# Two reorderings in the second block: low parts of two weight chunks around the query norms, and the router's first products ahead of the experts

## What is computed

```
hc, hx = context and latent tokens, scaled and shifted       # 256 + 256 tokens
proj   = h @ w_in            # parts: q, k|v, xbc (1536 columns), dt, z
q      = rope(rms_norm(q))   # 16 heads
xs|B|C = silu(conv5(xbc));  dt = softplus(dt_raw + dt_bias)
y      = state space scan of (xs, B, C, dt), both directions
o      = attention(q, k, v);  x = layer_norm(alpha*x + g_a * [y, o] @ w_out)
h      = x * (1 + sc_f) + sh_f
g      = h @ w_rg + b_rg;  e = h @ w_re + b_re           # router: 4 + 16 columns
weights of the 16 experts = top group, then top 2 of its 4 experts
out    = layer_norm(alpha*x + g_f * sum_e (silu(h@gate_e) * (h@up_e) * weight_e) @ down_e)
```

## Time and profile before

| what | us |
|---|---|
| median of 3 runs | 1785.45 (1785.32 to 1785.61) |
| the profiled execution, its own time | 1781.5 |
| its span, first to last instruction | 1779.5 |
| PE busy | 1640.4 (92%) |
| DVE busy | 1142.4 (64%) |
| ACT busy | 798.8 (45%) |
| POOL busy | 251.5 (14%) |
| mean granted TensorE clock | 0.954 |

### The profile page before, as it was taken

The page is one execution under the profiler, slowest core; times in us unless marked ns, Lnnn a source line. Parts: engine busy times, 40 slices in busy tenths (PEclk is TensorE's granted clock), DMA queues, the critical chain, the costliest instruction groups (busy, mean ns, idle before and its releaser), DMA issues. The chain is left out here.

```text
span 1779.5 us, 27095 instructions
## 1 busy us (share of the span) xinstructions
PE 1640.4 (92%) x10920; PEld 1412.4 (79%) x10920; DVE 1142.4 (64%) x1530; ACT 798.8 (45%) x1099; POOL 251.5 (14%) x287
## 2 busy tenths in 40 slices
PE   7999999899998999999899989898998868999996
PEld 5887898799976888889799976684565657899995
DVE  4669997566645669997566634767448564455555
ACT  4355554455533465554555424333227433343331
POOL 0200004144301200004254200103220000000000
PEclk9999999999999999999999999899869978999998
DMA  6554454465553545445465554221100222454541
GB/s 259 184 196 170 185 190 178 173 241 215 188 206 141 199 170 200 166 167 189 178 237 213 190 189 175 71 95 71 48 1 1 92 98 95 166 187 172 186 187 71
DMA packets 40123, 282.09 MB, mean 159 GB/s; under 512 B 4816, under 2 KB 5072, under 8 KB 6864
## 3 DMA queue, kind: packets, MB, share of 16 engines
q1 hardware_dynamic: 38432, 273.15, 41.4%
q10 hardware_dynamic: 1584, 7.42, 1.2%
HBM read 279.50 MB, written 1.05 MB: 158 GB/s over the span
## 5 line engine op out<-in xcount | busy, mean ns | idle before, releaser
L429 DVE TENSOR_TENSOR ring_low<-ring,sb_hi 128x2048 fp32r<-128x2048 f32 x116 | 271.0, 2336 | 180.4 <-ACT sb_hi L424 180.2
L424 ACT ACTIVATE sb_hi<-ring 128x2048 fp32r<-128x2048 f32 x116 | 222.5, 1918 | 278.2 <-DMA ring<-weights 121.2
L578 PE MATMUL psum<-sb_hS,sb_hi 128*128 128x256 f32 x704 | 202.2, 287 | 9.7 <-DVE ring_low L429 9.5
L581 PE MATMUL psum<-sb_hS,sb_hi 128*128 128x256 f32 x704 | 198.8, 282 | 0.0
L582 PE MATMUL psum<-sb_hS,ring_low 128*128 128x256 f32 x704 | 198.1, 281 | 0.0
L840 PE MATMUL psum<-sb_hfT,ring_low 128*128 128x256 f32 x704 | 196.8, 280 | 0.0
L1848 DVE TENSOR_TENSOR sb_split<-ring,sb_split 128x2048 fp32r<-128x2048 f32 x48 | 109.9, 2292 | 104.3 <-ACT sb_split L1843 104.3
L2229 PE MATMUL psum<-sb_hfS,sb_split 128*128 128x256 f32 x512 | 146.1, 285 | 6.1 <-DVE sb_hfS L2834 3.9
L578 PEld LDWEIGHTS psum<-sb_hS,sb_hi 128*128 128x128 f32 x704 | 133.1, 189 | 20.1 <-DVE ring_low L429 13.0
L2232 PE MATMUL psum<-sb_hfS,sb_split 128*128 128x256 f32 x512 | 145.4, 284 | 0.0
L2233 PE MATMUL psum<-sb_hfS,sb_split 128*128 128x256 f32 x512 | 145.4, 284 | 0.0
(11 more groups left out here) (435 smaller groups left out, 4103.7 us busy)
## 6 DMA issues: line engine op xcount, KB each, us to landing
ring<-weights SPq DMA_DIRECT2D x256, 1024.0 KB, 4.8
sb_rows_ffn<-rows ACTq DMA_DIRECT2D x4, 512.0 KB, 4.3
sb_rows_mix<-rows ACTq DMA_DIRECT2D x2, 1024.0 KB, 7.5
sb_rows<-rows ACTq DMA_DIRECT2D x1, 2048.0 KB, 9.8
sb_x<-x_in SPq DMA_DIRECT2D x2, 512.0 KB, 5.8
sb_y<-ctx_in SPq DMA_DIRECT2D x1, 1024.0 KB, 5.6
out<-sb_x SPq DMA_DIRECT2D x2, 512.0 KB, 2.6
sb_const<-const SPq DMA_DIRECT2D x1, 711.0 KB, 13.3
```

The lines of the kernel that those rows point to most:

```text
L424: act.activation(hi_of(n), ring[:, c % SLOTS, :], ACT.Copy).then_inc(hi_ready, 1)
L429: eng.tensor_tensor(low_of(n), ring[:, SPLIT_CHUNKS[n] % SLOTS, :], hi_of(n).bitcast(F32), ALU.subtract).then_inc(lo_dve, 1)
L578: mm = pe.matmul(out, hi[:, k, bs], hS[:, 0, k, :], start=(k == 0), stop=False)
L581: pe.matmul(out, hi[:, k, bs], hS[:, 1, k, :], start=False, stop=False)
```

## The change

In the inner projection, the low part of chunk 6 moves on DVE from behind `q_norm(1)` to between the two query norms. The high and low parts of chunk 7 move ahead of the dt chain: on ACT behind the k and v copies, on DVE directly behind `q_norm(1)`. At the experts, `strips("routeS")` moves on PE from behind gate 0 to ahead of the wait for the last low part of `hf`, with waits for the four drains of `hf`; `strip_sums("route")` moves from n = 2 to n = 1; ACT copies `routeS` ahead of the high part of expert chunk 2; DVE makes the low part of expert chunk 3 behind the router's logits and not ahead of them. No instruction is added or removed apart from waits.

```
--- before.py
+++ after.py
@@ -2210,6 +2210,10 @@
                 pe.wait_ge(x_normed, t + 1)
                 for c in range(2):
                     transpose4(("hf", c, t), [x[:, t, (4 * c + i) * P:(4 * c + i + 1) * P] for i in range(4)])
+            for t in range(TT):
+                for c in range(2):
+                    jobs.wait_drained(pe, ("hf", c, t))
+            strips("routeS", "w_r", hf)
             pe.wait_ge(h_lo, 4)
             pe.sem_inc(hid_used, 2)
 
@@ -2257,8 +2261,6 @@
             def experts(step):
                 for n, (part, e) in enumerate(MOE_ORDER):
                     if isinstance(step, int) and n == 1:
-                        strips("routeS", "w_r", hf)
-                    if isinstance(step, int) and n == 2:
                         strip_sums("route", wx[:, 0, 0:T], "routeS", TT, 20)
                     if isinstance(step, int) and n == 4:
                         weights_of_tokens()
@@ -2343,13 +2345,14 @@
             act.activation(expA, R("alog"), ACT.Exp).then_inc(a_ready, 1)
             for i in range(SEQ_TILES):
                 copy_out(("kv", i), kv[:, i, :])
+            weight_hi(act, 7)
             act.wait_ge(dt_neg, 1)
             act.activation(tmp_b[:, :, :], tmp_b[:, :, :], ACT.Exp).then_inc(dt_exp, 1)
             act.wait_ge(dt_u, 1)
             act.activation(tmp_a[:, :, :], tmp_a[:, :, :], ACT.Ln).then_inc(dt_ln, 1)
             for b in range(DX + 1):
                 if b < DX:
-                    if b % 2 == 0 and b < DX - 2:
+                    if b % 2 == 0 and 2 <= b < DX - 2:
                         weight_hi(act, 7 + b // 2)
                     jobs.wait_filled(act, ("xbc", b))
                     dst = xbc_xs[:, b, :] if b < 8 else bcf[:, b - 8, :]
@@ -2450,8 +2453,8 @@
             for c in range(2):
                 jobs.wait_drained(act, ("hf", c, 1))
                 high_part(1, c)
+            copy_out("routeS", wx[:, 0, 0:T], jobs.out("routeS")[:, 0:T])
             split_hi(act, 0, 2)
-            copy_out("routeS", wx[:, 0, 0:T], jobs.out("routeS")[:, 0:T])
 
             def silu(step, e):
                 wait_expert(act, step, "G", e, "filled")
@@ -2594,8 +2597,9 @@
             weight_lo(dve, 5)
             dve.wait_ge(params, 32)
             q_norm(0)
+            weight_lo(dve, 6)
             q_norm(1)
-            weight_lo(dve, 6)
+            weight_lo(dve, 7)
             jobs.wait_filled(dve, "dt")
             jobs.drain(dve.tensor_tensor(dtr[:, :, :], jobs.out("dt")[:, 0:128].rearrange("p (i h) -> p i h", i=4),
                                          bc(R("dtb").unsqueeze(1), [P, 4, 32]), ALU.add), "dt")
@@ -2837,7 +2841,6 @@
             dve.sem_inc(hid_hi, 2)
             dve.sem_inc(hid_ready, 2)
             split_lo(dve, 0, 2)
-            split_lo(dve, 0, 3)
 
 
             jobs.wait_filled(dve, "route")
@@ -2863,6 +2866,7 @@
             chain(dve.tensor_reduce(es[:, :, :], r32[:, :, :, :].rearrange("p t g e -> p t e g"), AX_X, ALU.add))
             chain(dve.tensor_reduce(r2b, es[:, :, :], AX_X, ALU.max))
             dve.tensor_tensor(es[:, :, :], es[:, :, :], bc(r2b.unsqueeze(2), [P, 2, 4]), ALU.subtract).then_inc(r_logits, 1)
+            split_lo(dve, 0, 3)
             dve.wait_ge(r_exp, 2)
             chain(dve.tensor_reduce(gs, r8a[:, :, :], AX_X, ALU.add))
```

## The result

| | before | after |
|---|---|---|
| median, us | 1785.51 (1785.32 to 1785.61, 4 runs) | 1769.86 (1767.49 to 1770.73, 4 runs) |
| profiled execution, us | 1781.5 | 1770.73 |
| its span, us | 1779.5 | 1768.6 |
| mean granted clock | 0.954 | 0.955 |

The ratio is 0.9911, with a 95% interval of 0.9898 to 0.9923: the change saves 15.6 us where 9.6 were forecast. The time lies 0.6 us under the range.

What follows compares the result with a forecast made beforehand. PE bounds the kernel, so gains come where it stands still or runs at the low clock. The sum -8.3 - 1.3 = -9.6 us gives 1771.9 for the profiled execution, plus 3.95 carried over: 1775.9, range 1770.5 to 1781.5.

Steps and rivals of the forecast that it cites:

- The stop of 8.2 us: Ahead of xbc 0, PE waits for the low part of chunk 6, late only by DVE's order; removing it: -8.2 us.
- The new stop ahead of xbc 3: Inner projection: PE waits from 1143.9 to 1145.8 for taps 0 to drain a region, +1.9 us, with no fall in clock.
- the twelve blocks: Xbc in the inner projection ends 8.3 us earlier: 8.2 + 2.5 - 1.9 - 0.5, bounds -6.7 to -8.7.
- Part two: Router's strips moved at the start of the experts: worth -1.3 us, between -0.5 and -2.1.
- The moved copy and low parts at the experts: ACT's strips copy delays chunk 2, and chunk 3's low part moves behind the logits; both hidden, with no cost.
- the router's earlier result: Router's chain on DVE ends at about 1483, but PE asks for its result only at 1491.89: buys nothing.
- The stop of 0.5 us at xbc 4: Inner projection: PE waits for the low part of chunk 8, behind ACT's Silu table load and high part, +0.5 us.
- The strips: Ahead of gate 0 they fit PE's wait with nothing to spare: 0 to 0.5 us, taken as +0.2.
- the half microsecond: At gate 0 the full clock returns sooner, -0.5 us; lost if products of 32 columns fare like transposes.
- the clock in the scan comes out otherwise: Rival: scan's clock shifts with fine timing; gain to 1771.9 (chance 0.11), or loss to 1782 to 1784 (0.08 with small gain).
- the lucky case: In the scan, the clock comes out better by 3.95 us, giving 1771.9; chance 0.11.
- The carried 3.95 us: Median of the runs lies 3.95 us above the profiled execution; this was added to 1771.9, giving 1775.9.

Runs made afterwards that it cites:

- both pairs: First pair: the profiled executions of the kernel before and the changed kernel, 1781.5 and 1770.73 us; second pair: e0_before and e1_after, one after the other on one chip.
- e8_lo6: The kernel before with only the low part of chunk 6 moved between the query norms: 1781.83 us, ratio 0.9981.
- e0_before: The kernel before, unchanged, run and traced again: 1785.1 us, ratio 1.0.
- e1_after: The changed kernel, unchanged, run and traced again: 1769.4 us, ratio 0.9912 to the kernel before.
- e2_part1: The kernel before with only the part of the diff that concerns chunks 6 and 7: 1771.52 us, ratio 0.993.
- e3_part2: The kernel before with only the part of the diff that concerns the router: 1783.46 us, ratio 0.999.
- e4: The kernel before with one unused 1.25 us multiply on DVE ahead of the copy of the cumulative sums: 1786.13 us, ratio 1.0006.
- e7: The changed kernel with two unused multiplies, 2.5 us, on DVE ahead of the copy of the cumulative sums: 1776.37 us, ratio 0.995 to the kernel before.
- e10_router_early: The changed kernel with the router's two transposes one chunk earlier, ahead of up 1: 1774.23 us, ratio 0.9934 to the kernel before.
- e6: The changed kernel with one unused 1.25 us multiply on DVE ahead of the copy of the cumulative sums: 1776.56 us, ratio 0.9946 to the kernel before.
- e9: The changed kernel with the first taps of block 0 ahead of the dt chain, on ACT and DVE: 1770.18 us, ratio 0.9919 to the kernel before.
- e11: The changed kernel with the edits of both e9 and e10_router_early: 1767.72 us, ratio 0.9903 to the kernel before.
- e12: The changed kernel with the second half of the dense z products and the ACT copies of z one unit later: 1773.3 us, ratio 0.9928 to the kernel before.
- e13: The kernel of e11 with the second half of the dense z products and the ACT copies of z one unit later: 1770.4 us, ratio 0.9915.

## Why the prediction was wrong

**Right, and shown.** The stop of 8.2 us was the order on DVE and nothing else, and it went. The clock of 1.00 was kept through it. The new stop ahead of xbc 3 measured 1.65 us for 1.9 worked out, and did not cost the clock. From the first matmul of block 2 to the first of xbc it took 8.3 us less in both pairs, and all of xbc came out 8.0 to 9.0 us shorter for 8.3; the twelve blocks themselves took 69.5 us before in the first pair and 68.5 in the second, which makes the difference. That chunk 7 had to move is shown by e8_lo6. The moved copy and low parts at the experts were hidden, and the router's earlier result bought nothing. Part two alone measured 1.3 us (1784.73 to 1783.46) for 1.3, within an interval of 0.2 to 3.4, so that this match is partly luck.

**Small errors.** The stop of 0.5 us at xbc 4 was charged for a table load that ACT does while it waits. The strips were charged 0.2 us and cost none. The full clock came back at gate 0 1.2 us sooner in the first pair and 3.3 us sooner in the second, which is worth half of that, 0.6 to 1.7 us for the 0.5 in the sum. PE at the start of gate 0, at the low clock, in e0_before, e1_after, e2_part1 and e3_part2:

```profile
1467.30:1472.00 4.70, 4.70 (x22) 0.51 0.02 5
...
1453.30:1454.70 1.40, 1.36 (x6) 0.50 0.06 18
...
1454.10:1458.90 4.80, 4.80 (x22) 0.50 0.02 5
...
1468.20:1469.50 1.30, 1.25 (x6) 0.50 0.06 19
```

So the half microsecond that products of 32 columns might have failed to win was won. The strips bring this, and not the earlier start of the stage: e2_part1 has the stage 13.2 us sooner than e0_before and no strips ahead of it, and the low clock lasts as long; e3_part2 has the strips and a start within 0.9 us of that of e0_before, and it is short. In the traces part two gives 1.9 to 2.7 us. Together the touched stages give 10.6 to 10.9 us, a miss of 1.0 to 1.3 on 9.6.

**What failed** is the term that the sum put at nothing, the clock in the scan. The sum of 9.6 us has no share for it, and the step that was to cover it, the rival "the clock in the scan comes out otherwise", had its gain and its chance too small. Its mechanism is the one that the runs show. I priced the lucky case by the 3.95 us between the profiled execution and the median, which came from elsewhere. The runs show 5.8 us for the scan, from the cumulative sums to the scores (123.0 us in e0_before, 117.2 in e1_after), of which the units give 7.8 and the stage ahead of them takes back 2.0. With 5.8 in place of 3.95 the lucky case is 1785.45 - 9.6 - 5.8 = 1770.05, and the measured median is 1769.86. The rows at hand gave a bound for the price: 26 us at clock 0.50 with PE busy throughout is up to 13 us of loss. The range, with its end at 1770.5, was cut for a price of 4.

I also gave the lucky change a chance of only 0.11, as if the long stretch were a property of the kernel. The delays of e4 to e7 leave the work of the units as it is and change when the scan begins, and with two multiplies the stretch of the kernel before falls away. So the start of the scan takes part in deciding it, and a shift of 8 us made the old stretch a poor guide. It does not decide alone: e10_router_early, unchanged ahead of the experts, mostly has the long one. Of the eight traces here in which xbc is over about 8 us sooner and the z products are in their place, four have the long stretch (the first of the changed kernel, e6, e7, e10) and four have not (e1, e2, e9, e11), so an even chance would have been nearer.

One reading of the rows was wrong as well. The stretches of rows 10 do not hold the same kinds of small products. PE from 1264 to 1287 us in the kernel before:

```profile
L1987 PE MATMUL psum<-ring,sb_hT 128*128 128x512 f32 x28 | 13.0, 616 | 0.0
```

These 28 products of 512 columns fill 13.0 of the 23 us, and from 1288 to 1314 there are none of them. So the rows did not show that fine timing alone decides; e12 and e13, which move half of such products, do change where the clock is low.

**The carried 3.95 us** was no constant either. The profiled execution of before had a fast block 1: it was over at 1072.6 us, and in the fourteen later traces at 1077.9 to 1081.3, with the same work. PE was busy there for 1005.5 us at a mean clock of 0.98 (7304 matmuls), and in e0_before for 1012.0 at 0.97 (7305), while its idle time was 67.1 and 66.2 us: the difference is the clock.

## What to carry to other kernels

Follow a removed stall through all queues to the next wait; that gave each of the touched stages here to within 1.3 us. Then look for long stretches in which PE is busy and the granted clock is 0.50: each is worth up to half its length, and a shift of 1 to 3 us ahead of it can win or lose a part of that (5.8 us here), so it belongs in the range with its full price. Count with it what the stage ahead gives back. A kernel with such a stretch has to be judged by several executions and by its stages, since one edit's own worth (here 10.6 us) and its time (15.6) can differ by half.

## What I had not expected of the hardware

- Added work can make a kernel faster. 2.5 us more on the critical path gave 1781.74 against 1784.79 us, ratio 0.9982 [0.9972, 0.9991], by a low-clock stretch in the scan that fell away (units of 75.3 us in e0_before, 73.8 with half the added work, 69.0 here).
- PE can be busy for 28.4 of 28.5 us at a mean clock of 0.52 (e0_before, 1290 to 1318.5). Almost all of its matmuls there have 32 rows or 64 columns; 7 of 512 columns and 8 transposes stand among them. It can also hold clock 1.00 while it is busy for only 11.76 of 16.00 us. The busy share alone says little about the clock.
- The Trainium skill (TensorE: Matmul & The Clock Gate, Part 4: PE-mode transpose) says that transposes do not bring on the full clock; no run here tests that by itself. Products of 32 columns do bring it on sooner: with the 16 strips ahead of gate 0 the low clock lasted 1.3 us into it (e3_part2), without them 4.7 and 4.8 us (e0_before, e2_part1), wherever the stage began.
